# A Fourier mix projection on 256 of 512 tokens: sums and differences of weight rows, plain fp32 matmuls

## The reference

```python
mod = silu(c) @ w_ada + b_ada                     # six vectors of 2048: sh1, sc1, ga1, sh2, sc2, ga2
h   = rmsnorm(x) * g_mix * (1 + sc1) + sh1
f   = fftn(h.reshape(512, 4, 512), axes=(0, 2), norm="ortho").real     # tokens, and channels of each group
x   = x + ga1 * (f.reshape(512, 2048) @ fno_w_out)                     # the mix projection
h2  = rmsnorm(x) * g_ffn * (1 + sc2) + sh2
x   = x + ga2 * (square(relu(h2 @ w_ffn_in)) @ w_ffn_out)              # 2048 -> 8192 -> 2048
out = rmsnorm(x) * g_final
```

## Time and profile before

| | |
|---|---|
| median of 3 runs | 1677.04 us (1675.62 to 1677.3) |
| the profiled execution | 1672.28 us, span 1670.5 us, mean granted clock 0.993 |
| TensorE, VectorE, ScalarE busy | 1624.9, 1258.1, 588.7 us |
| bytes moved | 272.66 MB, mean 163 GB/s |

### The profile page before, as it was taken

The page is one execution under the profiler, slowest core; times in us unless marked ns, Lnnn a source line. Parts: engine busy times, 40 slices in busy tenths (PEclk is TensorE's granted clock), DMA queues, the critical chain, the costliest instruction groups (busy, mean ns, idle before and its releaser), DMA issues.

```text
span 1670.5 us, 19246 instructions
## 1 busy us (share of the span) xinstructions
PE 1624.9 (97%) x7437; PEld 1324.2 (79%) x7437; DVE 1258.1 (75%) x1154; ACT 588.7 (35%) x701; POOL 16.2 (1%) x29
## 2 busy tenths in 40 slices
PE   6999999999999999999999999999999999999995
PEld 5667787788888888888888888888888888888874
DVE  6657798438888888886868686867777777777777
ACT  5341232453333323333333333333333333333333
POOL 0000000100000000000000000000000000000000
PEclk9999999999999999999999999999999999999998
DMA  9988999923535353432323232222222323232342
GB/s 356 371 333 329 373 348 344 359 90 101 201 101 201 101 201 110 167 108 94 124 77 126 87 114 100 101 100 100 100 100 100 102 99 119 82 126 76 126 177 101
DMA packets 94894, 272.66 MB, mean 163 GB/s; under 512 B 4304, under 2 KB 5632, under 8 KB 80896
## 3 DMA queue, kind: packets, MB, share of 16 engines
q1 hardware_dynamic: 91616, 249.91, 41.5%
q0 software_dynamic: 3088, 22.04, 3.8%
q10 hardware_dynamic: 144, 0.07, 0.0%
HBM read 263.61 MB, written 8.39 MB: 163 GB/s over the span
## 4 chain that ended last, share of the span: by engine, by line
PE 85%; DVE 6%; DMA 5%; ACT 2%; issue 1%; SPq 0%; ACTq 0%; DVEq 0%
PE banks L1270 16%; PE banks L1271 16%; PE banks L1272 16%; PE banks L1519 11%; PE banks L1521 11%; PE banks L1523 11%; DMA raw<-in_w_mix 3%; DVE wsp L908 1%; DVE acc_b L802 1%; PE banks L1288 1%; ACT wsp L513 1%; DMA raw<-in_w_ada 1%; PE banks L1452 1%; DVE xmix L1195 0%; DMA xres<-in_x 0%
## 5 line engine op out<-in xcount | busy, mean ns | idle before, releaser
L665 ACT ACTIVATE stp<-raw 128x1024 fp32r<-128x1024 f32 x330 | 343.2, 1054 | 524.6 <-PE banks L1272 233.9
L1100 DVE TENSOR_TENSOR stp<-raw,stp 128x1024 fp32r<-128x1024 f32 x330 | 402.0, 1222 | 157.8 <-ACT stp L665 155.0
L1270 PE MATMUL banks<-acts,stp 128*128 128x512 f32 x1024 | 399.5, 390 | 0.0
L1271 PE MATMUL banks<-acts,stp 128*128 128x512 f32 x1024 | 398.4, 389 | 0.0
L1272 PE MATMUL banks<-acts,stp 128*128 128x512 f32 x1024 | 398.4, 389 | 0.0
L1519 PE MATMUL banks<-stp,hid 128*128 128x512 f32 x840 | 326.8, 389 | 0.0
L1521 PE MATMUL banks<-stp,hid 128*128 128x512 f32 x840 | 326.8, 389 | 0.0
L1523 PE MATMUL banks<-stp,hid 128*128 128x512 f32 x840 | 326.8, 389 | 0.0
L1121 DVE TENSOR_TENSOR dacc<-dacc,banks 128x1024 f32<-128x1024 f32 x202 | 245.3, 1214 | 15.0 <-PE banks L1523 15.0
L1272 PEld LDWEIGHTS banks<-acts,stp 128*128 128x128 f32 x1024 | 192.2, 188 | 40.0
L1270 PEld LDWEIGHTS banks<-acts,stp 128*128 128x128 f32 x1024 | 192.3, 188 | 39.7 <-DVE acts L1043 0.2
(11 more groups left out here) (167 smaller groups left out, 1353.9 us busy)
## 6 DMA issues: line engine op xcount, KB each, us to landing
raw<-in_w_ada SPq DMA_DIRECT2D x80, 1024.0 KB, 7.5
raw<-in_w_ffn_in SPq DMA_DIRECT2D x64, 1024.0 KB, 5.8
raw<-in_w_ffn_out SPq DMA_DIRECT2D x64, 1024.0 KB, 5.0
raw<-in_w_mix SPq DMA_DIRECT2D x16, 1024.0 KB, 7.0
gate_w<-in_w_ada POOLq DMA_DIRECT2D x16, 1024.0 KB, 5.2
xres<-in_x SPq DMA_DIRECT2D x4, 1024.0 KB, 9.4
xmix_d<-xres POOLq DMA_DIRECT2D x4, 1024.0 KB, 9.5
xmix<-xmix_d SPq DMA_DIRECT2D x4, 1024.0 KB, 8.2
```

The costliest lines, as they stand in the source:

```text
L665: nc.scalar.activation(stp[:, slot, 0, :, :], source.rearrange("p (a n) -> p a n", a=2), ACT.Copy).then_inc(w_hi, 1)
L1100: nc.vector.tensor_tensor(stp[:, slot, 1, :, :], source.rearrange("p (a n) -> p a n", a=2), stp[:, slot, 0, :, :].bitcast(F32), ALU.subtra ...
L1270: nc.tensor.matmul(bank, w_hi_ap, m_hi, start=first, stop=False)
L1271: nc.tensor.matmul(bank, w_hi_ap, m_lo, start=False, stop=False)
```

## The change

Channels k and -k of a group are taken together. With E the cosine part and O the sine part of a token, a token t and its mirror -t have the values E - O and E + O on channel k, and swapped on -k. Their sum over the two weight rows is E (w[k] + w[-k]) -+ O (w[k] - w[-k]). So the projection is made for 256 tokens only, even and odd part by itself, with half the channels each, and the parts are added and subtracted behind it.

- The host puts the tokens of x and of the token table in the order 0 to 255, 256, 511 down to 257, and back at the end. The mix weight keeps channels 1 to 256 and 511 to 257 of each group; row 0 of each group is a small input of its own, loaded by GpSimd's queue at the start (`w0`, 4 by 2048), and a row of zeros takes its place.
- SP loads mix blocks into four buffers of their own (`mixw`), at the same places of the order; blocks 0 and 1 wait for the token transform, 2 and 3 for the channel transform, later ones for the unit four before on TensorE. The ring `raw` holds the other units alone.
- The third cosine tile, `four_tile`, the splitting into `fo`, the mirror copies, the high and low halves of the mix weight are gone. ScalarE copies even and odd part to `fe` and `fd`. Eight matmuls per group with a weight of 4 columns (`pick_r`) sum channel 0.
- VectorE makes difference and sum of the weight rows in place (`mix_sums`), two operations of 1024 columns.
- TensorE does a unit with ten plain fp32 matmuls of 512 columns (13 in the last unit of a block): even and odd part for two token tiles, and a one-row product for token 256.
- After a block ScalarE copies the even part out, VectorE adds and subtracts the odd part (`combine`), and then updates x. The last block goes by pairs of tiles (`update_pairs`).

The diff, cut to what the prediction speaks of:

```diff
+        mix_after.append(len(units) - SHIFT_LAST * (i == 0))
...
+        fe = place("fe", [P, F_TILES, HALF], F32, at_acts)
+        fd = place("fd", [P, F_TILES, HALF], F32, at_acts, skip=F_TILES * HALF)
+        w0 = place("w0", [GROUPS, D], F32, at_acts, skip=2 * F_TILES * HALF)
+        f0 = place("f0", [GROUPS, HALF], F32, at_acts, skip=2 * F_TILES * HALF + D)
...
+        mixw = [place(f"mixw{i}", [P, UK, COLS], F32, at, skip=skip) for i, (at, skip) in
+                enumerate(((at_w, 2 * UNIT), (at_w, 3 * UNIT), (at_hid, UNIT), (at_hid, 2 * UNIT)))]
...
+            def load_mix(n):
+                d, q = mix_units[n]
+                if n < 2:
+                    sp.wait_ge(spec_sum, DT)
+                elif n < MIX_SLOTS:
+                    sp.wait_ge(chan_sum, F_TILES)
+                else:
+                    sp.wait_ge(w_used, n - MIX_SLOTS + 1)
+                sp.dma_start(mixw[n % MIX_SLOTS][:, :, :],
+                             mix_v[:, UK * q:UK * (q + 1), COLS * d:COLS * (d + 1)])\
+                    .then_inc(mix_full[n % MIX_SLOTS], 16)
             for u, w in enumerate(units):
+                if u in mix_after:
+                    load_mix(mix_after.index(u))
...
+                    i = 2 * g + h
+                    act.wait_ge(chan_sum, i + 1)
+                    nc.scalar.activation(fe[:, i, :], banks[:, 2 * h, 0:HALF], ACT.Copy).then_inc(f_done, 1)
+                    nc.scalar.activation(fd[:, i, 1:HALF], banks[:, 2 * h + 1, 1:HALF], ACT.Copy).then_inc(f_done, 1)
...
+            act.wait_ge(first_sum, 1)
+            nc.scalar.activation(f0[:, :], banks[0:GROUPS, 6, 0:HALF], ACT.Copy).then_inc(f0_done, 1)
...
+            def even_copy(d):
+                act.wait_ge(w_used, (DT // UK) * (d + 1))
+                if d >= 1:
+                    act.wait_ge(x_updated, d)
+                b = 4 * (d % 2)
+                nc.scalar.activation(gated[:, 0:2, :], banks[:, b:b + 2, :], ACT.Copy).then_inc(even_out, 1)
...
+            for tt in range(2):
+                if tt == 0:
+                    act.wait_ge(pair_sum, 1)
+                else:
+                    act.wait_ge(w_used, MU)
+                nc.scalar.activation(gated[:, tt, :], banks[:, 4 + tt, :], ACT.Copy).then_inc(even_out, 1)
+            block_squares(1, DB - 1, DB, (0, 2))
+            block_squares(1, DB - 1, DB, (1, 3))
...
-            def four_tile(i):
...
+            def mix_sums(n):
+                tile = mixw[n % MIX_SLOTS]
+                dve.wait_ge(mix_full[n % MIX_SLOTS], 16 * (n // MIX_SLOTS + 1))
+                nc.vector.tensor_tensor(tile[:, 2:4, :], tile[:, 0:2, :], tile[:, 2:4, :],
+                                        ALU.subtract).then_inc(w_sum, 1)
+                dve.wait_ge(w_sum, n + 1)
+                nc.vector.scalar_tensor_tensor(tile[:, 0:2, :], tile[:, 0:2, :], 2.0, tile[:, 2:4, :],
+                                               ALU.mult, ALU.subtract).then_inc(w_lo, 1)
+            for g in range(2, GROUPS):
+                spec_low(g)
+            mix_sums(0)
...
+                sums = banks[:, 7, 0:FT * P].rearrange("p (b g r) -> p g b r", b=FT, g=GROUPS)
+                shifted, nyq = (two_tokens[:, i, :] for i in range(2))
+                by_group = lambda tile: tile.rearrange("p (g b) -> p g b", g=GROUPS)
+                nc.vector.tensor_tensor(by_group(shifted), by_group(fe[:, :, 0]), sums[:, :, 0:2, 0],
                                         ALU.add).then_inc(token_step, 1)
...
+            def combine(d):
+                dve.wait_ge(w_used, (DT // UK) * (d + 1))
+                b = 4 * (d % 2)
+                dve.wait_ge(even_out, d + 1)
+                nc.vector.tensor_tensor(gated[:, 2:4, :], gated[:, 0:2, :], banks[:, b + 2:b + 4, :],
+                                        ALU.add).then_inc(combined, 1)
+                dve.wait_ge(combined, d + 1)
+                nc.vector.tensor_tensor(gated[:, 0:2, :], gated[:, 0:2, :], banks[:, b + 2:b + 4, :],
+                                        ALU.subtract).then_inc(y_read, 1)
...
+            def update_pairs():
                 d = DB - 1
...
+                cols = slice(COLS * d, D)
+                dve.wait_ge(x_updated, d)
+                for tt in range(2):
+                    if tt == 0:
+                        dve.wait_ge(pair_sum, 1)
                     else:
...
+                        dve.wait_ge(w_used, MU)
+                    both = gated[:, tt:TT:2, :]
+                    dve.wait_ge(even_out, d + tt + 1)
+                    nc.vector.tensor_tensor(gated[:, 2 + tt, :], gated[:, tt, :], banks[:, 6 + tt, :],
+                                            ALU.add).then_inc(combined, 1)
+                    dve.wait_ge(combined, d + tt + 1)
+                    nc.vector.tensor_tensor(gated[:, tt, :], gated[:, tt, :], banks[:, 6 + tt, :],
+                                            ALU.subtract).then_inc(y_read, 1)
+                    dve.wait_ge(y_read, d + tt + 1)
+                    nc.vector.tensor_tensor(both, both, gate[:, cols].unsqueeze(1).to_broadcast([P, 2, COLS]),
+                                            ALU.mult).then_inc(gate_times, 1)
+                    dve.wait_ge(gate_times, d + tt + 1)
+                    nc.vector.tensor_tensor(xres[:, tt:TT:2, cols], xres[:, tt:TT:2, cols], both,
+                                            ALU.add).then_inc(pair_updated, 1)
...
+                if n == COMBINE0:
+                    combine(0)
...
+                        pe.wait_ge(pick_set, 2 + GROUPS)
                         for d in range(GT):
...
+                            for part in range(2):
+                                mm = nc.tensor.matmul(banks[0:GROUPS, 6, 0:HALF], pick_r[:, g, :],
+                                                      modp[:, (g + 1) % 2, part, d, 0:HALF],
+                                                      start=(g == 0 and d == 0 and part == 0),
+                                                      stop=(g == GROUPS - 1 and d == GT - 1 and part == 1))
+                        if g == GROUPS - 1:
+                            mm.then_inc(first_sum, 1)
...
+                for k in range(DT):
+                    mm = nc.tensor.matmul(banks[0:GROUPS, 4, 0:32], pick[:, k // GT, :], shift32[:, k, :],
+                                          start=(k == 0), stop=(k == DT - 1))
...
+            def even_part(n, tt):
+                d, q = mix_units[n]
+                tok, cols = slice(P * tt, P * (tt + 1)), slice(COLS * d, COLS * (d + 1))
+                bank = banks[:, 4 * (d % 2) + tt, :]
+                for i in range(2):
+                    mm = nc.tensor.matmul(bank, fe[:, 2 * q + i, tok], mixw[n % MIX_SLOTS][:, i, :],
+                                          start=(q == 0 and i == 0), stop=False, skip_group_check=True)
+                if q == GROUPS - 1:
+                    mm = nc.tensor.matmul(bank, f0[:, tok], w0[:, cols], start=False, stop=True, skip_group_check=True)
+                return mm
...
+            def odd_part(n, tt):
+                d, q = mix_units[n]
+                tok = slice(P * tt, P * (tt + 1))
+                for i in range(2):
+                    mm = nc.tensor.matmul(banks[:, 4 * (d % 2) + 2 + tt, :], fd[:, 2 * q + i, tok],
+                                          mixw[n % MIX_SLOTS][:, 2 + i, :], start=(q == 0 and i == 0),
+                                          stop=(q == GROUPS - 1 and i == 1 and tt == 1), skip_group_check=True)
+                return mm
...
+            def row_part(n):
+                d, q = mix_units[n]
+                row = banks[0:1, 4 * (d % 2) + 2, :]
+                for i in range(2):
+                    mm = nc.tensor.matmul(row, w_two[:, 2 * q + i:2 * q + i + 1], mixw[n % MIX_SLOTS][:, i, :],
+                                          start=False, stop=False, skip_group_check=True)
+                if q == GROUPS - 1:
+                    mm = nc.tensor.matmul(row, w_first[:, :], w0[:, COLS * d:COLS * (d + 1)], start=False, stop=True,
+                                          skip_group_check=True)
+                return mm
...
+                if n == 0:
+                    even_part(n, 1)
+                    shift_end()
+                    odd_part(n, 1)
+                    odd_part(n, 0)
+                    patch()
+                    even_part(n, 0)
+                    mm = row_part(n)
+                elif n < MU - 1:
+                    even_part(n, 0)
+                    odd_part(n, 0)
+                    row_part(n)
+                    even_part(n, 1)
+                    mm = odd_part(n, 1)
+                else:
+                    even_part(n, 0)
+                    late_step(1)
+                    odd_part(n, 0)
+                    row_part(n).then_inc(pair_sum, 1)
+                    late_step(2)
+                    even_part(n, 1)
+                    late_step(3)
+                    mm = odd_part(n, 1)
```

(41 more changed lines are left out.)

246 lines of the change are left out of this document (79 added, 167 removed).

## The result

| | before | after |
|---|---|---|
| median | 1676.71 us (5 runs) | 1666.64 us (5 runs) |
| ratio, 95% interval | | 0.9943 [0.9928, 0.9957] |
| profiled execution, span | 1672.28, 1670.5 us | 1665.92, 1663.7 us |
| busy TensorE, VectorE, ScalarE | 1624.9, 1258.1, 588.7 us | 1606.9, 1252.8, 551.5 us |

What follows compares the result with a forecast made beforehand. TensorE was taken as the bound, transfers and VectorE nearly as full. Start, VectorE's stretch, unit 15 and tail put the reduction 8.5 us earlier, less 2.5 for the clock: 6 us, 1666.3 profiled, 1671.0 median; range 1664 to 1681.

Steps and rivals of the forecast that it cites:

- The bound: Mix stage: TensorE never rests, transfers and VectorE nearly as full; halving TensorE's work gives only what those two leave.
- Start of the stage: Last SHIFT1 load to first vector product: landed 115.2, turned rows 130.7, VectorE free 131.9 (was 135.88); bounds 129.5 and 137.5.
- The four fp32 matmuls: Before the turned rows: four plain fp32 matmuls replace twelve fp32r ones, 4.5 us (3.5 at full clock, 6.9 at half).
- The tiny products: Before the turned rows: 16 new tiny fp32 products on TensorE, taken as 1.5 us, between near zero and 3.6.
- the eight small VectorE operations: Behind the turned rows, before VectorE is free: eight operations of 0.16 us, 1.2 us.
- VectorE's operations: Mix stage: 1.22 and 1.25 us per unit, combinations +7.3; 150.3 us, 153.5 with waits and hitches, last sum at 285.4.
- TensorE's unit: Mix units 1 to 14: 8.6 us each, 11.2 for a block's last; 132 us in all, inside VectorE's 150.
- Unit 15: Last mix unit with interposed steps: 15.4 us, starting 1.5 us late, ending at 302.3 (before 314.5).
- The tail: Last mix matmul to reduction: 6.0 us (before 2.4), reduction at 308.3; then 2.5 us lost to a lower clock.
- Transfers: Mix stage: 49 loads, 136 us, covered by 12 us; rival that they bind at 333 GB/s: 1677, chance 0.22.
- The sum: Whole kernel: 6 us earlier, 1666.3 for the profiled execution, 1671.0 for the median; forecast's chance 0.58.
- The clock: Rival: clock falls at each mix unit's start, 3.3 us a unit, 12 instead of 8.6; about 1702, chance 0.08.

Runs made afterwards that it cites:

- ve_less: Changed kernel without the second VectorE operation on each mix block (sum of the weight rows): 1656.4 us, 0.9898 of the kernel before.
- te_less: Changed kernel without the one-row products of the eleven units 1 to 14 that don't end a block: 1666.28 us, 0.9958 of the kernel before.
- load_less: Changed kernel with half of each mix block loaded from block 4 on: 1667.0 us, 0.9963 of the kernel before.
- b_te_less: Kernel before with two instead of three matmuls per product in mix units 1 to 14: 0.9974 of the kernel before.
- b_ring: Kernel before with mix blocks 1 to 15 in two buffers of their own outside the shared ring: 0.9991 of the kernel before.
- b_ring_te: Kernel before with two own buffers for mix blocks 1 to 15 and two matmuls per product in units 1 to 14: 1659.64 us, 0.9917.
- both_less: Changed kernel without the second VectorE operation per mix block and without one-row products in units not ending a block: 1656.69 us, 0.9905.

## Why the prediction was right

**The bound.** Right. It said that TensorE was the engine that never rests, that ring and VectorE stood directly behind it, and that VectorE takes over: its last sum at 285.4, measured 283.7. `ve_less`, `te_less` and `load_less` show that VectorE is the bound now, `b_te_less`, `b_ring` and `b_ring_te` that two resources had to be released.

**Start of the stage.** Forecast 115.2, 130.7 and 131.9 for the last SHIFT1 load, the turned rows and VectorE; measured 116.69, 130.04 and 130.74. The load took 6.7 us, not 5.3. The four fp32 matmuls took 3.44, not 4.5, at a granted clock of 1.00 in 120:128, where the earlier trace rows had 0.59; TensorE had been idle 0.98 and 0.72 us before them. The tiny products took 0.93, not 1.5, and the eight small VectorE operations 0.70, not 1.2, since they overlap. The terms miss both ways, and that the start was met within 1.2 us is in part luck; it moves by some 2 us either way between executions. Its upper bound, 137.5, is 1.1 us more than the terms add up to (115.2 + 14.45 - 5.0 + 6.9 + 3.6 + 1.2), and nothing hangs on it.

**VectorE's operations.** 1.22 us for the scalar_tensor_tensor of 1024 columns (1.25 forecast), 1.21 and 1.22 for the combination (1.214). The stretch of 153.5 us was measured at 153.0, but by other parts: 149.05 us busy where the sum had 150.3, and 3.95 us of seams and waits where it had 3.2.

**TensorE's unit: mis-sized.** I took 0.86 us a matmul from the row sums. Here each line is two matmuls of two instructions, and the distance of the starts is their price:

```profile
264.84 1.88 PE L1395 MATMUL banks<-mixw,fe 128*128 128x512 f32 x4
266.56 1.88 PE L1406 MATMUL banks<-mixw,fd 128*128 128x512 f32 x4
268.37 1.88 PE L1416 MATMUL banks<-mixw,w_two 128*1 128x512 f32 x4
270.18 1.98 PE L1395 MATMUL banks<-mixw,fe 128*128 128x512 f32 x4
272.00 1.88 PE L1406 MATMUL banks<-mixw,fd 128*128 128x512 f32 x4
```

From even to odd part it is 1.72 us, 0.86 each as forecast. Around the one-row product it is 1.81 three times, 0.1 us more each. So a unit takes 8.87 us, not 8.6. A block's last unit, with three more matmuls and more such changes, takes 12.3 (153.37 to 165.68), not 11.2, and units 1 to 14 with the row sums take 138 us, not 132. In `te_less`, in the units without one-row products, all pairs start 1.72 apart. TensorE did not wait about 1 us for each unit: it waited four times, 8.1 us in all where I gave 18, and 6.4 of them in one wait. Unit 15 took 17.0 us, not 15.4 (its 13 matmuls 12.5, not 11.2), but it began 0.15 us behind the last sum, not 1.5. The two errors nearly cancel, which is luck: 283.74 + 17.15 = 300.9, against 285.4 + 16.9 = 302.3.

**The tail.** 6.0 forecast, 6.2 measured (300.9 to 307.13). The clock did fall behind it: 0.60 in 308:312, some 1.6 us, 2.5 forecast. 1.4 us of the distance to the relu went there.

**Transfers.** I called them covered by 12 us of reserve, at 378 GB/s. The reserve was nearer to 9 us by `ve_less` and `both_less`, at 395 GB/s. The rival didn't come true, but it stood right behind the forecast.

**The sum.** Forecast 6 us: 1666.3 for the profiled execution, where 1665.92 was measured, and 1671.0 for the median, where 1666.64 was. The traces have 8.4 us at matched points. The 2.4 us between are the start (1.2), the stretch on VectorE (0.5) and the clock behind the tail (1.1), less 0.5 for unit 15 and the tail. That the profiled execution was met within 0.4 us is luck: the 1.6 us lost to the clock at the very end and the 0.4 us around the span hid most of the miss. By the medians the change gave 10.1 us, and 6 us is a ratio of 0.9964, just outside the first interval and inside the second.

**The clock.** The rival had the clock fall at the start of each unit. Its condition did not come about in the changed kernel, with four waits; behind the one of 6.4 us four instructions took 3.78 us where others took 1.98, and the mean of 136:280 was 0.98. `te_less` comes nearer to it: nine waits, 24.5 us, a mean of 0.94. Behind its waits of 2.37, 6.01 and 8.23 us the first four instructions took 3.3 to 3.8 us, behind one of 2.43 they took 1.98. The stage was no longer for it, since TensorE had the slack. So the price is real at single places, about 1.8 us on those four instructions, and not the 3.3 us at each of 15 units. The forecast read 64:72, with 5.34 of 8 us busy, as agreeing in part with the warning that it quotes; a clock of 1.00 there speaks against it.

## What to carry to other kernels

When an engine is busy all the time in a stage, look who stands right behind it before halving its work: here relief of TensorE alone was worth 4 us, of the ring alone 1 to 2, of both 14. An engine's idle time in front of a ring slot is a bound in waiting. And read a matmul's price from rows with the same mix of products as the new code: the change between full and one-row products, which no row of the kernel before had, cost 0.1 us each time.

## What the runs showed of the hardware that I had not expected

- Plain fp32 matmuls of 512 columns start 0.86 us apart, in the row sums and also where the stationary matrix changes with each (1.72 us for two). A one-row product costs at least as much as a full one, and around it the distance is 1.81 us for two.
- The transfers of one core reached 395 to 397 GB/s over 144 us at a share of 0.99, where 352 at 0.93 had looked close to full.
- After the same 2.17 us of work in 4 us the granted clock of the next 4 us was 1.00 in one execution and 0.65 in another, 1.6 us: part of the spread between executions that no edit explains. So is the start of the mix stage, which lay between 129.1 and 133.6 us in ten executions.
